# Moving two norm scales from the rows that enter the projections to the results that leave them

## The reference

```python
def rms_norm_2(x, g):
    xf = x.astype(jnp.float32)
    y = xf * lax.rsqrt(jnp.mean(xf * xf, axis=-1, keepdims=True) + EPS)
    return (y * g.astype(jnp.float32)).astype(x.dtype)

def even_mixer(hn, ...):
    proj = hn @ w_in
    xr, yr, q, k, v, f_logit = jnp.split(proj, EVEN_SPLITS, axis=-1)
    xc = causal_depthwise_conv(xr, conv_w, conv_b)
    h_lru = rglru(xc, ...)
    y_a = h_lru * jax.nn.gelu(yr)
    log_f = jax.nn.log_sigmoid(f_logit + f_b)
    y_b = fox_attention(q, k, v, log_f)
    return jnp.concatenate([y_a, y_b], axis=-1) @ w_out

def odd_mixer(hn, ...):
    q, k, v, g, lr = jnp.split(hn @ w_in, ODD_SPLITS, axis=-1)
    log_a = jax.nn.log_sigmoid(lr @ gate_w2 + gate_b) / GLA_TAU
    o = gla_chunked(q * dk ** -0.5, k, v, log_a)
    ...                                   # head norm, then o * silu(g), then @ w_out
```

## Time and profile before

| | |
|---|---|
| median of three runs | 1960.36 us (1958.73 to 1962.9) |
| profiled execution, device time | 1962.08 us |
| its span, first to last instruction | 1958.8 us |
| TensorE busy in the span | 1918.3 us, 98% |
| VectorE busy | 1185.5 us, 61% |
| ScalarE busy | 969.5 us, 49% |
| first transition (last output product to first product of xr) | about 638 to 656 us |
| second transition (last product of SwiGLU to first product of gq) | about 957 to 971 us |
| stretch of the experts | about 1105 us to the end |

### The profile page before, as it was taken

One profiled execution on the slowest core, in us unless ns is written; L12 is line 12 of the kernel. 1 busy time (PEld: TensorE's weight loads), 2 busy tenths in 40 slices (PEclk: granted clock), 3 DMA queues, 4 the chain that ended last, 5 costly groups with the idle time before them and its releaser, 6 DMA issues.

```text
span 1958.8 us, 30650 instructions
## 1 busy us (share of the span) xinstructions
PE 1918.3 (98%) x12361; PEld 1570.0 (80%) x12361; DVE 1185.5 (61%) x1698; ACT 969.5 (49%) x1429; POOL 29.8 (2%) x29
## 2 busy tenths in 40 slices
PE   6999999999999999999999999999999999999998
PEld 4999899999899989999999736883588887368833
DVE  4767886565785776666663217951498884059611
ACT  3647753466863575443463206740476673057501
POOL 1000000000000120000000000000000000000000
PEclk7999999999999999999999999999999999999999
DMA  9985556465544542555455899999999999999997
GB/s 291 270 267 184 163 174 160 98 188 189 158 140 140 177 142 88 194 194 158 158 187 203 336 395 407 416 365 412 409 413 409 404 374 347 414 408 411 409 410 303
DMA packets 292565, 536.83 MB, mean 274 GB/s; under 512 B 67076, under 2 KB 198600, under 8 KB 278096
## 3 DMA queue, kind: packets, MB, share of 16 engines
q1 hardware_dynamic: 287968, 530.82, 75.4%
q10 hardware_dynamic: 3920, 3.69, 0.6%
q0 software_dynamic: 544, 0.43, 0.1%
HBM read 533.83 MB, written 1.07 MB: 273 GB/s over the span
## 4 chain that ended last, share of the span: by engine, by line
PE 62%; DMA 2%; DVE 1%; ACT 1%; issue 0%; SPq 0%; DVEq 0%
PE bank L803 14%; PE bank L805 14%; PE bank L804 13%; PE bank L1603 9%; PE bank L1630 4%; DMA pool<-in_od_exp_w 2%; PE bank L1411 1%; PE bank L1458 1%; PE bank L1487 1%; PE bank L1519 1%; PE bank L763 1%; PE bank L748 1%; PE bank L1616 0%; PE bank L788 0%; PE bank L779 0%
## 5 line engine op out<-in xcount | busy, mean ns | idle before, releaser
L3123 DVE TENSOR_TENSOR expert_lo<-pool,w_hi 128x2048 fp32r<-128x2048 f32 x168 | 376.9, 2287 | 46.6 <-ACT w_hi L2268 46.5
L2268 ACT ACTIVATE w_hi<-pool 128x2048 fp32r<-128x2048 f32 x168 | 313.2, 1912 | 29.4 <-DMA pool<-in_od_exp_w 25.3
L803 PE MATMUL bank<-h_upper,upper 128*128 128x256 f32 x1056 | 310.0, 294 | 2.1 <-DVE ring_lo L2537 2.0
L804 PE MATMUL bank<-h_lo,upper 128*128 128x256 f32 x1056 | 300.5, 285 | 0.0
L805 PE MATMUL bank<-h_upper,ring_lo 128*128 128x256 f32 x1056 | 300.4, 284 | 0.0
L2537 DVE TENSOR_TENSOR ring_lo<-ring,upper 128x1024 fp32r<-128x1024 f32 x148 | 179.7, 1222 | 102.9 <-ACT upper L1785 102.6
L803 PEld LDWEIGHTS bank<-h_upper,upper 128*128 128x128 f32 x1056 | 204.1, 193 | 9.6 <-issue 8.5
L804 PEld LDWEIGHTS bank<-h_lo,upper 128*128 128x128 f32 x1056 | 204.3, 193 | 1.0 <-issue 0.4
L805 PEld LDWEIGHTS bank<-h_upper,ring_lo 128*128 128x128 f32 x1056 | 204.1, 193 | 0.0
L1603 PE MATMUL bank<-pool,xe_light 128*64 128x512 f32 (+1 forms) x976 | 187.4, 539 | 2.8 <-issue 2.0
L2847 DVE TENSOR_TENSOR piece_lo<-ring,piece_hi 128x1024 fp32r<-128x1024 f32 x118 | 144.7, 1237 | 73.9 <-ACT piece_hi L1774 73.6
(11 more groups left out here) (482 smaller groups left out, 3605.0 us busy)
## 6 DMA issues: line engine op xcount, KB each, us to landing
pool<-in_od_exp_w SPq DMA_DIRECT2D x330, 1024.0 KB, 13.9
ring<-in_w_in SPq DMA_DIRECT2D x48, 1024.0 KB, 5.7
ring<-in_ev_ffn_w SPq DMA_DIRECT2D x33, 1024.0 KB, 5.3
ring<-in_w_ada SPq DMA_DIRECT2D x24, 1024.0 KB, 7.7
ring<-in_od_w_in SPq DMA_DIRECT2D x12, 1024.0 KB, 5.4
ring<-in_ev_w_in SPq DMA_DIRECT2D x10, 1024.0 KB, 5.4
ring<-in_w_in SPq DMA_DIRECT2D x32, 256.0 KB, 4.5
ring<-in_w_out SPq DMA_DIRECT2D x8, 1024.0 KB, 4.9
```

Source lines behind the costliest of these rows:

```text
L803: nc.tensor.matmul(b, left[0], right[0], start=first, stop=False, skip_group_check=True)
L804: nc.tensor.matmul(b, left[0], right[1], start=False, stop=False, skip_group_check=True)
L2268: nc.scalar.activation(w_hi[q % HIS], ring_slot(q), ACT.Copy)\
L3123: V.tensor_tensor(low_slot(q), ring_slot(q), w_hi[q % HIS].bitcast(F32), ALU.subtract)\
```

## The change

The rows that enter the projections are no longer multiplied by the norm's scale. They are only multiplied by the norm's weights, pair by pair right behind the sum that makes x, and their upper and lower parts are formed at once. The first four tiles (xr, in the first mixer) or two tiles (gq 0 and 1, in the linear attention) run chunk by chunk in `project_weighted`: for each chunk of rows all tiles' products, then that chunk's sum of squares. The scale is known behind them. It is spread in the middle of the flog (or lr) product, ScalarE copies it to SBUF (`row_root`), and every projection result is multiplied by it on VectorE as it leaves its bank (the new `rows_out`, counted by the new semaphore `scaled_rows`), where ScalarE copied before. vf and gv, whose tokens lie on partitions, are scaled by ScalarE in two instructions instead of one. The gates gg go through SBUF (`h`) before the tanh. The first four pieces are formed during the output projection of the first block. The tile `yo` moves to another place.

```diff
-        token_squares(("mix", 0))
-        keep_busy(4)
-        spread(("mix", 0), 0, NT, h_ready, "mix", 0, KD - 1)
-        keep_busy(5)
+        def project_weighted(key, *targets, squares="attn"):
+            banks = [claim("gemm", (name, c), scaled_rows, name, c) for name, c, _ in targets]
+            for k in range(KD):
+                pe.wait_ge(left_ready, when(left_ready, *key, k))
+                for b, (name, c, tile) in zip(banks, targets):
+                    w = take_piece((tile,), c % 2, KD, P)
+                    m = product(b[:, 0:S], [t[:, k] for t in w], (left_hi[:, k], left_lo[:, k]), k == 0, k == KD - 1)
+                    if k == KD - 1:
+                        m.then_inc(psum_ready, wrote(name, c))
+                        release_piece((tile,), c % 2)
+                mean_square_part(key, k, squares)
+
+        project_weighted(("mix", 0), *(("xr", c, "xr" + "1" * (c // 2)) for c in range(4)))
         pe.wait_ge(flog_spread, when(flog_spread, "all"))
-        chunk(("flog",), "gemm", clog_ready, ("flog",), KD, lambda k: flogw[:, k], lambda k: h[:, k],
-              fresh=("mix", 0))
+        b = claim("attn", ("flog",), clog_ready, "flog_rows")
+        for k in range(KD):
+            if k == KD // 2:
+                spread(("mix", 0), 0, NT, rstd_row, "mix", 0, group="attn")
+            m = nc.tensor.matmul(b[:, 0:S], flogw[:, k], h[:, k], start=(k == 0), stop=(k == KD - 1))
+        m.then_inc(psum_ready, wrote("flog"))
...
-        token_squares(("mix", 1))
-        keep_busy(6)
-        spread(("mix", 1), 0, NT, h_ready, "mix", 1, KD - 1)
-        keep_busy(6)
+        project_weighted(("mix", 1), ("gq", 0, "gq"), ("gq", 1, "gq"), squares="gemm")
...
+                if (name, c) not in (("gq", 0), ("gq", 1)):
+                    project_piece((name + "1" * (c // 2),), c % 2, (name, c), scaled_rows)
+                if (name, c) == ("gq", 2):
+                    pe.wait_ge(scaled_rows, when(scaled_rows, "lr"))
...
+                if l == L - 1 and 2 < c < KD - 1:
+                    piece_upper(c - 3)
...
+        for c in range(0, KD, 2):
+            act.wait_ge(x_ready, when(x_ready, "l", L - 1, c + 1))
+            nc.scalar.activation(sq[:, c:c + 2], x[:, c:c + 2], ACT.Square).then_inc(sq_ready, two(sq_ready, "mix", 0, c))
+            act.wait_ge(weighted_step, when(weighted_step, "l", L - 1, c + 1))
+            nc.scalar.activation(left_hi[:, c:c + 2], h[:, c:c + 2], ACT.Copy)\
+                .then_inc(left_hi_ready, two(left_hi_ready, "mix", 0, c))
         token_root("mix", 0)
-        pair_uppers(("mix", 0))
-        for n in range(2, PIECES):
-            piece_upper(n)
+        piece_upper(PIECES)
+        row_root("mix", 0, slot=0)

         act.wait_ge(psum_ready, when(psum_ready, "ms", "mix", 0))
         fetch(loaded_block2, mask, C["causal"][:, 0:P])
...
-        for c in range(4):
-            copy_out(("xr", c), conv[:, c, 3:3 + S])
+        for c in range(1, 4):
             piece_upper(c + PIECES)
...
+        inverse_tokens("mix", 0)
+        piece_lower(PIECES)
         link(V.memset(conv[:, :, 0:3], 0.0))
-
+        dve.wait_ge(rstd_row, when(rstd_row, "mix", 0))
+        def rows_out(name, c, *dsts):
+            key = (name,) if c is None else (name, c)
+            b = psum(dve, *key)
+            for rows, dst in dsts:
+                m = V.tensor_tensor(dst, b[rows, 0:S], rstd[rows, 0], ALU.mult)
+            m.then_inc(scaled_rows, tick(scaled_rows, *key))
...
+        for c in range(4):
+            rows_out("xr", c, (every, conv[:, c, 3:3 + S]))
+        piece_lower(1 + PIECES)
         b = psum(dve, "flog")
-        V.tensor_scalar(clog, b[:, 0:S], fb, None, ALU.add).then_inc(clog_ready, tick(clog_ready, "flog"))
+        V.tensor_tensor(clog, b[:, 0:S], rstd[:, 0], ALU.mult).then_inc(clog_ready, tick(clog_ready, "flog_rows"))
+        dve.wait_ge(clog_ready, when(clog_ready, "flog_rows"))
+        V.tensor_scalar(clog, clog, fb, None, ALU.add).then_inc(clog_ready, tick(clog_ready, "flog"))
...
         for c in range(4):
-            piece_lower(c + PIECES)
+            if c > 1:
+                piece_lower(c + PIECES)
             convolve(c)
...
         for n in range(4, 8):
+            rows_out("yr", n - 4, (every, yr[:, n - 4]))
             piece_lower(n + PIECES)
...
+        rows_out("gq", 0, (every, gq[:, 0]))
+        rows_out("gq", 1, (every, gq[:, 1]))
+        piece_lower(GQ0 - 1 + PIECES)
+        rows_out("lr", None, (slice(0, 16), lr[0:16, :]))
+        rows_out("gq", 2, (every, gq[:, 2]))
...
+        rows_out("gq", 3, (every, gq[:, 3]))
         piece_lower(GQ + 3 + PIECES)
+        rows_out("gk", 0, (every, gk[:, 0]))
         piece_lower(GQ + 4 + PIECES)
```

More of the change, by code:

```diff
@@ L227, in two_blocks @@
     table = place(12, 384)
-    z = {b: place(4, S) for b in "abc"}
+    yo = place(8, S)
+    z = {"a": yo[:, 0:4], "b": yo[:, 4:8], "c": place(4, S)}
     cq_flat = place(3 * S)
@@ L772, in token_squares, with spread @@
             m.then_inc(psum_ready, wrote("ms", *key))
-        def spread(key, first, n, freed_by, *step):
+        def spread(key, first, n, freed_by, *step, group="gemm"):
             pe.wait_ge(rstd_ready, when(rstd_ready, *key))
-            b = claim("gemm", ("r", *key, first), freed_by, *step)
+            b = claim(group, ("r", *key, first), freed_by, *step)
             for t in range(n):
@@ L1291, in _ @@
             busy[4 + n] = (x_ready, when(x_ready, "ffn", 2 * n + 1))
-        token_squares(("mix", 1))
-        keep_busy(6)
-        spread(("mix", 1), 0, NT, h_ready, "mix", 1, KD - 1)
-        keep_busy(6)
+        project_weighted(("mix", 1), ("gq", 0, "gq"), ("gq", 1, "gq"), squares="gemm")
         w = take("lr")
-        chunk(("lr",), "gemm", proj_ready, ("lr",), KD, lambda k: w[:, k], lambda k: h[:, k], rows=16, fresh=("mix", 1))
+        b = claim("attn", ("lr",), scaled_rows, "lr")
+        for k in range(KD):
+            if k == KD // 2:
+                spread(("mix", 1), 0, NT, rstd_row, "mix", 1, group="attn")
+            m = nc.tensor.matmul(b[0:16, 0:S], w[:, k], h[:, k], start=(k == 0), stop=(k == KD - 1))
+        m.then_inc(psum_ready, wrote("lr"))
         release("lr")
@@ L2128, in fox_v @@
             b = psum(act, "vf", j)
-            nc.scalar.activation(vf[:, :, 256 * j:256 * j + 256], b.rearrange("p (t n) -> p t n", t=NT), ACT.Copy)\
-                .then_inc(proj_ready, tick(proj_ready, "vf", j))
+            for t in range(NT):
+                m = nc.scalar.activation(vf[:, t, 256 * j:256 * j + 256], b[:, 256 * t:256 * t + 256], ACT.Copy,
+                                         scale=rtok[:, t:t + 1])
+            m.then_inc(proj_ready, tick(proj_ready, "vf", j))
             for n in range(2):
@@ L2527, in gate, with piece_lower, left_lower, weighted @@
                 .then_inc(z_ready, tick(z_ready, name, *key))
+        def piece_lower(n):
+            if n >= len(pieces):
+                return
+            dve.wait_ge(piece_hi_ready, when(piece_hi_ready, n))
+            src = piece_source(n)
+            hi, lo = piece_tiles(n, *src.shape[1:])
+            V.tensor_tensor(lo, src, hi.bitcast(F32), ALU.subtract).then_inc(piece_ready, tick(piece_ready, n))
+            freed_at[where[pieces[n][0]]] = (piece_ready, ticks.counts["piece_ready"])
+        def left_lower(key, k, src, into=(left_hi, left_lo)):
+            dve.wait_ge(left_hi_ready, when(left_hi_ready, *key, k))
+            V.tensor_tensor(into[1][:, k], src, into[0][:, k].bitcast(F32), ALU.subtract)\
+                .then_inc(left_ready, tick(left_ready, *key, k))
+        def weighted(weight, c, *ready):
+            dve.wait_ge(x_ready, when(x_ready, *ready, c))
+            V.tensor_scalar(h[:, c], x[:, c], weight, None, ALU.mult)\
+                .then_inc(weighted_step, tick(weighted_step, *ready, c))
+        def after_sum(c):
+            if c >= 0:
+                for k in (c, c + 1):
+                    weighted(vec("norm_mix_2", k), k, "l", L - 1)
+            if c > 0:
+                pair_lower(("mix", 0), c - 2)
+            if c == KD - 2:
+                pair_lower(("mix", 0), c)
+        def pair_lower(key, c):
+            pair = slice(c, c + 2)
+            dve.wait_ge(left_hi_ready, when(left_hi_ready, *key, c + 1))
+            V.tensor_tensor(left_lo[:, pair], h[:, pair], left_hi[:, pair].bitcast(F32), ALU.subtract)\
+                .then_inc(left_ready, two(left_ready, *key, c))
         def lower(*tiles):
@@ L2828, in _ @@
                 shift_gain(1)
+            if l == L - 1:
+                for n in range(PIECES - 1):
+                    piece_lower(n)
             inverse_tokens("post", l)
+            if l == L - 1:
+                dve.wait_ge(psum_ready, when(psum_ready, "out", l, KD - 1))
+                piece_lower(PIECES - 1)
             r = spread_root("post", l)[:, 0:S]
@@ L3023, in _ @@
```

(18 more changed lines are left out.)

108 lines of the change are left out of this document (46 added, 62 removed).

## The result

| | before | after |
|---|---|---|
| median | 1960.36 us (13 runs, 1956.27 to 1963.68) | 1977.1 us (13 runs, 1965.1 to 1981.87) |
| profiled execution | 1962.08 us | 1979.26 us |
| its span | 1958.8 us | 1977.2 us |
| mean granted clock of the span | 0.988 | 0.984 |

The changed kernel is slower by 16.7 us; the ratio is 1.0084, with a 95% interval from 1.0069 to 1.0099. The direction was forecast, the size was not: 1967.5 was predicted, and 1977.1 lies above the range.

A forecast was written before the change was run, and what follows sets the result against it. TensorE, busy 98%, was taken as the bound, with the experts set by their weight stream from 1110 us. First transition +6.0, second 0, clock +1.1 gave +7.1 us, moving the median from 1960.4 to 1967.5; range 1959 to 1972.

The forecast's parts named there:

- The clock, second transition: Linear attention's transition: a 3.4 us low stretch would meet products, costing 0 to 1.7 us; 1.1 taken.
- nothing won without the clock: Linear attention's transition: 2.2 us won on TensorE, but gk 3 and gv 0 wait; gv 0 within 0.3 us of before.
- The clock, first transition: Gaps of 3, 3.9 and 3.3 us likened to one of 2 us that kept full clock: 0, range 1.7.
- The hold by nine issues: First transition, ScalarE: piece 5's upper part stands behind nine transfer issues lasting 5.8 us; 3.9 us lost before yr 1.
- Flog and two convolutions in front of piece 6: First transition, VectorE: they stand ahead of piece 6, ready at 678.5 where yr 2 wants it at 675.2; 3.3 us lost.
- Pieces 7 and 8: First transition: piece 7 comes behind convolution 2, 0.1 us lost; piece 8 behind convolution 3 and a yr result, 0.7 lost.
- The chunkwise start: First transition: xr's products start at 647.3, chunks take 1.8 us, yr 0 starts at 665.5 instead of 667.6; 2.1 won.
- Behind the gates: After qf 0: waits at gates, vf and first attention head same as before; up to 0.9 us for GpSimd in range.
- The gates gg: Linear attention: one step more per gate; the output product's last chunk is wanted at 2.7 us, ready at 2.2; no cost.
- A: Rival: nine issues don't hold back piece 5; first transition's loss shrinks to 0.9 us, about 1962.4; chance 16%.
- B: Rival: pieces 5 and 6 arrive in time, gk 3 and gv 0 not held; 4.3 us faster, 1956.1; chance 12%.
- C: Rival: low clock also meets first-transition products or those behind the new gaps; +1.7, GpSimd 0.9; 1970 or above; 12%.

The follow-up runs named there:

- t1_alone: Against before, only the first transition's part of the change, with the linear attention's norm as before; 1973.4 us, ratio 1.0072.
- t2_hold: Against after, 13 matmuls of no use fill the gap ahead of gq 0 in the second transition; 1968.24 us, ratio 1.0044.
- t1_hold: Against after, 26 useless matmuls instead of 12 between the spread and the first product of xr in the first transition; 1974.81 us.
- fetch_behind: Against after, ScalarE's nine transfers of the first transition moved behind the upper parts of pieces 5, 6 and 7; 1973.51 us.
- t2_squares_behind: Against after, the second transition's eight sums of squares run behind all 48 products of gq 0 and gq 1; gap left; 1974.14 us, ratio 1.0064.
- all_four: Against after, transfers behind the upper parts, VectorE's order by due time, and useless matmuls in both gaps; 1965.61 us, ratio 1.0027.
- qf_late: Against all_four, ScalarE copies qf out of its banks unscaled, as before, and VectorE scales it out of SBUF behind the gates; 1959.89 us, ratio 1.0001.
- t2_alone: Against before, only the linear attention's norm is changed; 1969.24 us, ratio 1.0047.
- qf_late_t2_order: Against qf_late, VectorE makes three lower parts around gq 3 before it takes out gk 0 in the linear attention; 1961.04 us, ratio 1.001.
- after_qf_late: Against after, only qf's way out is put back to ScalarE, with its scaling behind the gates; 1977.37 us.
- due_order: Against after, VectorE's order by due time: pieces 6 to 9 ahead of the convolutions they stood behind; 1978.54 us.

## Why the prediction was wrong in size

By stages the trace of after stands 19.5 us above before, where the sum of the prediction was 7.1. (The medians stand 16.7 apart, and the forecast of the median was off by 9.6.) The 12.4 between them are 8.9 in the linear attention's transition, 2.6 up to the first gate product, 2.2 at the gates and 0.2 behind, less 1.6 for a low stretch of before that is gone.

**The clock, second transition.** This step failed. It took the low stretch as long as in before, 3.4 us, and left two thirds of its half on products: +1.1, at most 1.7. Measured were 20.5 us at the lower level and 9.4 us (72.14 less 62.76). The low stretch of before (963.3 to 966.7) had met `keep_busy` and the spread, as rows 9 let one see: lr only starts at 967.16. The new work behind the gap was thin, and under it the stretch lasted. The length seen once was no constant even for the same work: in t1_alone, whose second transition is that of before, it was 6.8 us. The prediction named "a clock of 0.50 in the chunkwise products" as what would show it wrong, and so it was. Its other statements on this transition held: gq 0 at 5.14 us behind the first row of x (4.95 reckoned); nothing won without the clock (+0.6 in t2_hold, 0 forecast), since gk 3 and gv 0 wait for VectorE, 0.61 and 0.53 where 1.0 and 0.8 stood; a chunk lasts 1.16 and not 1.06.

**The clock, first transition.** Taken as 0 with 1.7 for the range, since gaps of 3 to 4 us were put nearer to the one of 2 us, the only gap that the rows held. Nothing measured stood behind that. It was 1.7, by t1_hold. A second low stretch, at 675, cost nothing: it made yr 1 last 4.6 us, but yr 2 waited for its piece anyway.

**The queues.** Right, to within half a microsecond for each wait. The hold by nine issues: 3.9 forecast, 4.35 from start to start in after, none left in fetch_behind. Flog and two convolutions in front of piece 6: 3.3 forecast, 3.2 measured (1.46 of it as a wait, the rest under the slow products). Pieces 7 and 8: 0.8 forecast, 0.8 measured. The chunkwise start: 6.42 us behind the spread forecast, 6.66 measured; a chunk lasts 1.88 us, not 1.8, 0.6 in all. The 2.1 us that this start was to win never came: yr 0 starts 27.0 us behind the spread where 24.6 was forecast and before has 26.7 (656.09 + 11.5 less 640.88), and with the gap filled 25.5 (t1_hold). To the first gate product +6.0 was forecast and +8.60 came, of which 1.7 is the clock and 0.6 the chunk.

**Behind the gates.** "The waits at the gates ... come to the same as before, and the 6 us stay": the stage came out 2.23 longer. The statement on the waits held, 0.53 + 1.47 for 2.00; without the low stretch of 3.4 us the stage is 0.6 longer (t1_hold, t2_squares_behind), inside the 0.9 left for GpSimd. The other 1.6 are the clock. What was not seen is that this balance holds only because TensorE comes so late: with the other waits gone (all_four) the stage costs 6.3 us, by waits for banks and a low stretch of 6.8 us about them, and both waits and stage shrink again when qf leaves by ScalarE (qf_late, 2.6). So the losses ahead were hiding this one.

**The gates gg.** Nothing forecast, nothing found: -1.56 is a low stretch of before that after lacks; it returns in t2_squares_behind (-0.01), which has the same gg code.

**Rivals.** A fell with fetch_behind. B needed VectorE and ScalarE shorter by 4 to 7 us; even with their queues put in order (qf_late) the first two stages come to +1.3. C, low clock on more of the products, at 1970, came nearest and had the right cause, but it too was priced by stretches of 3.4 us.

**Still open.** Why a low stretch comes at the gates in after, t1_alone, t2_alone, t2_hold, qf_late and qf_late_t2_order, and not in before, fetch_behind, t1_hold, t2_squares_behind or after_qf_late, which stand idle there for about as long, was not found. Whether the change makes it likelier is open too. One of after's 13 runs took 1965.1 us at a mean clock of 0.991 (the others 0.983 to 0.987). Against the middle of the others, 0.985, that is an estimated 24 us less at the lower level (0.006 x 1965 / 0.5), and 12 us less time. Only the stretch of 20.5 us is of that size in the trace of after, though the first 600 us also vary by 14 us; the run has no trace, so whether the long stretch can fail to come isn't known.

## What to carry to other kernels

A low stretch of TensorE's clock is to be priced by the work that follows it: ask which matmuls run behind the gap, and how thin they are, not how long the last such stretch was. Where work is moved to start earlier in a gap, fill the gap with matmuls; letting dense products come first gave back only 4.5 of 9.4 us here, since the thin work behind them lowered the clock again. And moving a scale from rows to results moves it onto the engine that frees the banks; look up for each bank when that engine comes to it, and whether the engine that used to copy had the time.

## What the runs showed of the hardware

A stretch with TensorE busy for 97% of the time stayed at the lower clock for 20.5 us in after (17.1 in t2_alone and due_order), while the same instructions ran at 1.00 in t2_hold. Sums of squares of one column, 32 in a row, lowered the clock while TensorE never stood (t2_squares_behind: sums from 976.74, the clock down from 979.8 to 986.6, busy 10.00 of 10.00 us from 978 to 988). Nine small transfers took 6.1 us of ScalarE's queue (666.04 to 672.13); moved behind three activations, the first five were issued beside them (0.37 us for one, 0.92 for two), and only the last four, of gate weights, held the queue.
